# Moving small loads and rotary angles beside the feed-forward, and the key compression and key turns into the key-value stage, on one core

## The chip, the cores and the metric

One core of a Trainium2 chip. The metric is device microseconds of one execution of the whole program, lower is better.

## The reference, cut to what matters

A deep fp32 network over 512 tokens of width 1024 (P = 128 partitions, so LT = 4 token tiles). Its last layers are a forgetting attention, a feed-forward, then shared keys and values, a sparse attention that uses them, and a second feed-forward. The part that matters here is `shared_kv`, between the first feed-forward and the sparse attention:

```python
def shared_kv(h, positions, kv_norm, kv_w, kc_pe, vc_pe, kc_w1, kc_w2, vc_w1, vc_w2, kc_gain, ks_gain, kw_gain):
    hn = rms_norm_2(h, kv_norm)
    parts = (hn @ kv_w).reshape(B, T, 6, N_KV_GROUPS, HEAD_DIM)     # 512 x 1024 @ 1024 x 768
    kc_raw, vc_raw, ks, vs, kw, vw = (parts[:, :, i] for i in range(6))
    starts = arange(31) * 16; idx = starts[:, None] + arange(32)     # 31 overlapping blocks of 32 tokens
    def compress(raw, pe, w1, w2):                                   # w1: 2048 x 256, w2: 256 x 64
        blk = (raw[:, idx] + pe)...reshape(B, 31, 2, 32 * 64)
        return gelu(blk @ w1) @ w2
    kc, vc = compress(kc_raw, kc_pe, kc_w1, kc_w2), compress(vc_raw, vc_pe, vc_w1, vc_w2)
    kc = partial_rope(rms_norm_2(kc, kc_gain), positions[:, ends])
    ks = partial_rope(rms_norm_2(ks, ks_gain), positions)
    kw = partial_rope(rms_norm_2(kw, kw_gain), positions)
```

(Here cut and abridged; two groups of heads, head size 64; the rotary part covers 16 of the 64.)

## The kernel before, in words

The program is a long row of stages. Each `Stage` opens a block with one instruction stream per engine (SP issues transfers, PE multiplies, ACT, DVE and POOL do the rest); the streams meet at its end, and the next stage starts after that. Within a stream the order is the order of the code; engines wait for each other on semaphores. `Chain` lets DVE wait for its own last instruction.

After the first feed-forward (`conv_ffn`, layer 0) `sparse_attention` (L3619) runs these stages in turn:

1. `vector_steps` at L3660: a memset of the positions.
2. `load_all` (L86): SP issues seven small loads (positions twice, inverse frequencies, signs, the compression's position terms `cmp_pe`, a mask, a bias) and the first two landings of `kv_w` (an `Early` object); ACT's queue issues the compression's weights `cmp_w` (two of 2048 KB, two of 64 KB). The stage ends when the seven small loads have landed.
3. `rope_from_positions` (L3392): twelve small DVE steps make the angles, ACT looks up sine twice, one DVE step puts the signs on.
4. `normed_linear` (L625) for `kv_w`: ACT squares and takes roots of the rows of x, DVE normalizes them, PE turns them, ACT and DVE make a high and a low part (fp32r) of the turned rows and of each 256-wide piece of the weights; PE multiplies hi*hi, hi*lo, lo*hi. Pieces 0 and 1 are the token-major columns 256 to 767 (keys and values, `KS`, `VS`, `KW`, `VW`), piece 2 the feature-major raw columns 0 to 255 that the compression needs. `hi_part`, `lo_part`, `keep_unit`, `head_square`, `head_sum`, `head_scale`, `head_rope` are its steps; per-head norm and rotary of KS and KW come in the loop over pieces and after it, with POOL multiplying the gains.
5. `load_all` (call at L3684): two transfers inside SBUF swap halves of `raw`, so that both groups lie on both halves of the partitions.
6. `compress` (L3443): sixteen DVE adds (L3474) lay out the blocks; PE (L3495) multiplies with the weights `w1` as the stationary side (128 columns) and the blocks as the moving side (62 columns), into `cmp_ps`; ACT takes gelu; then two small products into `kc_ps` and `vc_ps`.
7. `head_norm` (L1039) of the compressed keys.
8. `turn_stacks` (L1195): POOL doubles each of six key stacks into `twice`, PE turns them (L1231), ACT and DVE make hi and lo.
9. `normed_linear` for `b_w_in`, the projection of the sparse attention; not touched, but for what comes below.

`conv_ffn` (L3244) has a norm stage (`norm_turn`, whose SP stream issues the `Early` loads) and a main stage of 66 chunks: 44 up (UP = 44) and 22 down. For chunk c + 2 ACT makes the high part of the weights (L3324) and DVE the low part (L3346), after PE has used chunk c - 1; PE multiplies chunk c. In the up part DVE also convolves and ACT takes silu.

In `mixture`, an earlier stage that the prediction uses for a price, L1982 multiplies fp32 with a stationary side of 64 columns, the two halves of the array's columns in turn, and a moving side of 512.

## Time and profile before

| what | value |
|---|---|
| median of 3 runs | 4573.47 us (4568.03 to 4594.96) |
| the profiled execution's own time | 4570.35 us |
| its span, first to last instruction | 4568.5 us |
| PE busy | 3857.8 us, 84% of the span |
| DVE busy | 2038.3 us, 45% |
| ACT busy | 1082.4 us, 24% |
| POOL busy | 561.4 us, 12% |
| mean granted TensorE clock | 0.898 |

Times of the trace are us from the span's start. A busy share is a mean over stages that have different limits, so the table says little of a change to one stage; the time lines of that stage do. The time of the profiled execution is 1.85 us more than its span.

### The profile page before, as it was taken

To read this page: it belongs to the slowest core of one execution; us is meant where nothing else is said; L and a number is where in the kernel's file an instruction comes from. 1 tells how busy PE (TensorE), PEld (TensorE's weight loads), DVE (VectorE), ACT (ScalarE), POOL (GpSimd) and SP (SyncE) were. 2 spreads that over 40 slices of the span, in tenths; PEclk is the share of its full clock that TensorE was granted. 3 is DMA by queue.
4 is the path that set the end of the run, shared out by engine and by line. 5 is a ranking of instruction groups with operands and counts; after the bars stand their busy time and mean duration, and the time that the engine had idled before them with its cause. 6 is when DMAs were issued, how large, how long until landed. Compare 5 with 4: busy or idle time off the path is not lost. (4 is left out here: it accounts for less than half of the span.)

```text
span 4568.5 us, 70879 instructions
## 1 busy us (share of the span) xinstructions
PE 3857.8 (84%) x29878; PEld 2815.9 (62%) x29878; DVE 2038.3 (45%) x3790; ACT 1082.4 (24%) x2119; POOL 561.4 (12%) x626
## 2 busy tenths in 40 slices
PE   6878876999978797979977877798899958798998
PEld 4645673444448674868953222396688748686877
DVE  3268953000044456756542000256477244554762
ACT  2122322000023413222111000225322122472221
POOL 0011000111102202414200000014000000250000
PEclk8987787999989997969788999999899977699999
DMA  4241017999951211000049999820122221002222
GB/s 153 85 156 30 1 61 315 383 395 389 396 168 54 88 64 39 3 1 3 2 156 399 397 401 401 327 75 20 56 96 93 79 72 39 19 2 76 95 93 79
DMA packets 194619, 657.94 MB, mean 144 GB/s; under 512 B 27544, under 2 KB 85912, under 8 KB 144620
## 3 DMA queue, kind: packets, MB, share of 16 engines
q1 hardware_dynamic: 176576, 613.95, 35.7%
q0 software_dynamic: 13056, 35.14, 2.9%
q8 instruction: 238, 3.90, 0.4%
q10 hardware_dynamic: 4672, 4.33, 0.3%
q14 instruction: 77, 0.63, 0.0%
HBM read 624.44 MB, written 28.39 MB: 143 GB/s over the span
## 5 line engine op out<-in xcount | busy, mean ns | idle before, releaser
L3346 DVE TENSOR_TENSOR w_lo<-ffn_landing,w_hi 128x1024 fp32r<-128x1024 f32 x132 | 161.4, 1225 | 293.3 <-ACT w_hi L3324 293.3
L3298 PE MATMUL ffn_ps<-ffn_inT_hi,w_hi 128*128 128x512 f32 x704 | 276.0, 392 | 9.3 <-DVE w_lo L3346 9.3
L3298 PE MATMUL ffn_ps<-ffn_inT_lo,w_hi 128*128 128x512 f32 x704 | 275.5, 391 | 0.0
L3298 PE MATMUL ffn_ps<-ffn_inT_hi,w_lo 128*128 128x512 f32 x704 | 275.3, 391 | 0.0
L1982 PE MATMUL up_ps<-w_quarter,rowsT 128*64 128x512 f32 x1024 | 237.2, 606 | 36.7 <-DMA w_quarter<-in_moe_w 36.7
L1982 PE MATMUL gate_ps<-w_quarter,rowsT 128*64 128x512 f32 x1024 | 237.0, 608 | 30.9 <-DMA w_quarter<-in_moe_w 22.2
L1982 PE MATMUL down_ps<-w_quarter,hiddenT 128*64 128x512 f32 x1024 | 235.2, 599 | 30.6 <-DMA w_quarter<-in_moe_w 28.5
L1898 POOL DMA_INDIRECT summed_dram<-gains_then_rows,part_row x48 | 74.8, 1559 | 932.3 <-DVE gains_then_rows L2112 927.4
L1982 PEld LDWEIGHTS down_ps<-w_quarter,hiddenT 128*64 128x64 f32 x1024 | 68.5, 136 | 188.4 <-issue 129.6
L2105 DVE TENSOR_TENSOR gain_then_hidden<-up_ps,gain_then_hidden 128x768 f32<-128x768 f32 (+1 forms) x32 | 26.4, 825 | 351.5 <-PE up_ps L1994 179.6
L1982 PEld LDWEIGHTS up_ps<-w_quarter,rowsT 128*64 128x64 f32 x1024 | 68.6, 138 | 182.7 <-issue 111.1
L3324 ACT ACTIVATE w_hi<-ffn_landing 128x1024 fp32r<-128x1024 f32 x132 | 138.1, 1049 | 181.5 <-PE ffn_ps L3311 163.4
L1982 PEld LDWEIGHTS gate_ps<-w_quarter,rowsT 128*64 128x64 f32 x1024 | 69.6, 139 | 178.6 <-issue 119.0
L2042 ACT ACTIVATE rowsT<-misc_ps 128x384 f32<-128x384 f32 (+1 forms) x64 | 27.8, 438 | 599.7 <-PE misc_ps L1971 598.0
L2112 DVE SCALAR_TENSOR_TENSOR gains_then_rows<-down_ps,part_gates,row_gain 128x512 f32<-128x512 f32 (+1 forms) x48 | 30.3, 659 | 308.6 <-PE down_ps L1994 170.1
L2098 DVE COPY hiddenT<-misc_ps 128x512 f32<-128x512 f32 (+1 forms) x48 | 27.4, 599 | 309.6 <-PE misc_ps L2012 309.6
L3298 PEld LDWEIGHTS ffn_ps<-ffn_inT_hi,w_hi 128*128 128x128 f32 x704 | 133.2, 189 | 37.5 <-DVE w_lo L3346 9.8
L3298 PEld LDWEIGHTS ffn_ps<-ffn_inT_hi,w_lo 128*128 128x128 f32 x704 | 133.1, 189 | 28.0
L3298 PEld LDWEIGHTS ffn_ps<-ffn_inT_lo,w_hi 128*128 128x128 f32 x704 | 133.2, 189 | 27.7
L1525 ACT ACTIVATE probT<-probT_ps 128x384 f32<-128x384 f32 (+3 forms) x256 | 112.0, 451 | 96.3 <-PE probT_ps L1483 94.7
L1656 DVE SCALAR_TENSOR_TENSOR mla_in<-mixedT,cv_w,mla_in 128x512 f32<-128x512 f32 x240 | 130.8, 612 | 0.0
L2773 PE MATMUL x_ps<-X_blocks,prod 64*64 64x64 f32 x1728 | 124.9, 229 | 5.6 <-ACT prod L2486 4.5
(693 smaller groups left out, 8831.5 us busy)
## 6 DMA issues: line engine op xcount, KB each, us to landing
w_quarter<-in_moe_w SPq DMA_DIRECT2D x384, 1024.0 KB, 17.4
ffn_landing<-in_f_w_up SPq DMA_DIRECT2D x88, 512.0 KB, 3.5
ada_ring<-in_ada_w SPq DMA_DIRECT2D x80, 512.0 KB, 5.2
ffn_landing<-in_f_w_down SPq DMA_DIRECT2D x44, 512.0 KB, 3.5
w_landing<-in_od_w_in SPq DMA_DIRECT2D x13, 1024.0 KB, 10.4
w_landing<-in_a_w_in SPq DMA_DIRECT2D x12, 1024.0 KB, 5.2
ada_landing<-in_ada_w SPq DMA_DIRECT2D x8, 1024.0 KB, 12.6
w_landing<-in_ev_w_in SPq DMA_DIRECT2D x6, 1024.0 KB, 5.2
```

Of the source, the lines that this page charges most:

```text
L1525: nc.scalar.activation(pT[:, i % ST, a:b], pt[k % 2][:, 0:b - a], ACT.Copy).then_inc(tkept, 1)
L1656: ins = nc.vector.scalar_tensor_tensor(out=to, in0=src, scalar=w[:, c, j:j + 1], in1=to, op0=ALU.mult, op1=ALU.add)
L1898: nc.gpsimd.indirect_dma_start(out=to, out_offset=bass.IndirectOffsetOnAxis(ap=pidx[:, part, e:e + 1], axis=0), in_=ys[e % 2][:, cols], in ...
L1982: mm = nc.tensor.matmul(out[n * 64:(n + 1) * 64, 0:LW], v[:, k, 0:LR], land[c][:, kk, n * LW:(n + 1) * LW], start=(k == 0), stop=(k == KD ...
L2042: nc.scalar.activation(xs[:, half * HK:(half + 1) * HK, :], misc[half][:, 0:HK * R].rearrange("p (k r) -> p k r", k=HK), ACT.Copy).then_in ...
L2098: nc.vector.tensor_copy(hT[:, :, r0:r0 + r].rearrange("p (n j) r -> p j n r", n=n), misc[part][:, 0:KD * r].rearrange("p (j n r) -> p j n ...
L2105: tt(hid[:, 0:W], p3[:, 0:W], hid[:, 0:W], ALU.mult).then_inc(hid_ready, 1)
L2112: last = nc.vector.scalar_tensor_tensor(out=ys[e % 2][:, cols], in0=py[:, cols], scalar=gall[:, part, e:e + 1], in1=g2r[:, cols], op0=ALU. ...
L2773: mm(bx[g][hb, cols], Pm[g][hb, q, :], X[g][hb, q, :], start=True, stop=True, skip_group_check=True)
L3298: mm = nc.tensor.matmul(ps[c % 4][:, :], w[:, c % NP, cols], h[:, k, :], start=(k + i == 0), stop=(k == KD - 1 and i == 2))
L3324: nc.scalar.activation(wh[:, c % NP, :], land[:, c % NL, :], ACT.Copy).then_inc(hi_ready, 1)
L3346: nc.vector.tensor_tensor(wl[:, c % NP, :], land[:, c % NL, :], wh[:, c % NP, :].bitcast(F32), ALU.subtract).then_inc(split, 1)
```

## The change

- A new class `Positions` makes the buffers and the memset before the first feed-forward. Its seven small loads are issued by SP in that feed-forward's norm stage, behind the four early weight landings (`Together`); the angle steps run on DVE behind the low part of chunk UP + 6 (loop index UP + 4), the two sine look-ups on ACT at UP + 6, the signs on DVE at UP + 10.
- `vector_steps`, `load_all` and `rope_from_positions` go from between the feed-forward and the key-value stage. `kv_w` and the compression's weights are loaded by SP inside that stage: pieces 0 and 1, the four loads of `guest.load`, then piece 2.
- The order of pieces is KS/VS, raw, KW/VW. `keep_raw` makes four copies of 64x512 per unit in place of two, straight to both halves, into the spare rows of x; the two swapping transfers go.
- A new class `Compress` is a guest of `normed_linear`: three memsets on DVE at the start (`clear`), the sixteen block adds on DVE after the keeps of piece 1 (`blocks`), doubling on POOL between the gains, and PE, ACT and DVE parts behind the stage's own. The first product has the sides swapped: blocks stationary (64 columns, the two inputs on the two halves of the array's columns), `w1` moving (256 columns), 32 products in place of 64. The hidden rows are then turned twice. The norm and rotary of the compressed keys (all on DVE but the root), and the six key turns, are inside too. `compress`, this use of `head_norm`, and `turn_stacks` for the keys go.
- `head_rope` gets one semaphore increment, in every `normed_linear` with rotary heads.

```diff
                 sp.dma_start(land[:, c % RING, :, 0:b - a], wv[:, :, job[1] + a:job[1] + b]).then_inc(landed[c % RING], 16)
+                if guest is not None and c == RING - 1:
+                    guest.load(sp)
...
+                if guest is not None:
+                    guest.double(pool, i)
...
+            if guest is not None:
+                guest.double_compressed(pool)
...
+                guest.tensor(pe)
...
+                guest.scalar(act)
...
+                    dve.sem_inc(head_roped, 1)
...
+                guest.clear(chain)
             for i in range(3):
...
+                if guest is not None and c == guest.after:
+                    guest.blocks(dve, kept, u)
                 lo_part(c + RING)
                 head_sum(c - 1)
                 head_scale(c - 2)
...
+                guest.vector(dve, chain)
...
+                  early=early if side is None else Together(early, side))
...
+                if side is not None and c == UP + 6:
+                    side.look_up(act)
...
+                if side is not None and c == UP + 4:
+                    side.angles(dve, chain)
+                if side is not None and c == UP + 10:
+                    side.signs(dve, chain)
...
+        self.pairs = [(pos[:, 0:LT], d["positions"].rearrange("(t p) -> p t", p=P)),
+                      (pos[0:NCMP, LT:n], d["positions"][31:SEQ:16].unsqueeze(1)),
+                      (self.inv[:, :], d["inv_freq"].partition_broadcast(P)),
+                      (self.sign[:, :], d["sin_sign"].partition_broadcast(P)), (self.pe_c[:, :, :], d["cmp_pe"]),
+                      (self.mask[:, :, :], d["cmp_mask"]), (self.bias[:, :], d["b_gate"].partition_broadcast(P))]
+        vector_steps(nc, lambda chain: nc.vector.memset(pos[:, :], 0))
...
+    def look_up(self, act):
+        act.wait_ge(self.ready, 1)
+        self.nc.scalar.activation(self.cos[:, :, :], self.b[:, :, :], ACT.Sin)
+        self.nc.scalar.activation(self.sin[:, :, :], self.a[:, :, :], ACT.Sin).then_inc(self.looked, 1)
...
+    def load(self, sp):
+        for dst, src in self.loads:
+            sp.dma_start(dst, src).then_inc(self.landed, 16)
+
+    def clear(self, chain):
+        chain(self.nc.vector.memset(self.blk[:, :, :, :, :], 0.0))
+        self.nc.vector.memset(self.zc, 0.0)
+        chain(self.nc.vector.memset(self.vb, 0.0))
...
+        ins.then_inc(self.ready, 1)
+
+    def double(self, pool, head):
+        if head == 0:
+            pool.wait_ge(self.ready, 1)
+        pool.wait_ge(self.roped, head + 1)
+        for i in (2 * head, 2 * head + 1):
+            src = self.stacks[i][0]
+            self.nc.gpsimd.tensor_copy(self.dup[i], src.unsqueeze(2).broadcast_to([P, LT, 2, 64])).then_inc(self.doubled, 1)
+
+    def double_compressed(self, pool):
+        pool.wait_ge(self.normed, 1)
+        for g in range(2):
+            pool.wait_ge(self.sturned, g + 1)
+            self.nc.gpsimd.tensor_copy(self.dup[g][:, 0:1], self.zc[:, 0:1, g, :].unsqueeze(2).broadcast_to([P, 1, 2, 64])) \
...
+        def stack(i):
+            n = LT if i < 4 else 1
+            pe.wait_ge(self.doubled, i + 1)
+            if i >= 2:
+                pe.wait_ge(self.skept, i - 1)
+            for t in range(n):
+                ins = turn(self.stack[i % 2][:, t * P:(t + 1) * P], self.dup[i % 4][:, t].rearrange("p y d -> p (y d)"),
+                           self.ident)
+            ins.then_inc(self.sturned, 1)
+
+        pe.wait_ge(self.landed, 16 * len(self.loads))
+        pe.wait_ge(self.ready, 1)
+        for m in range(16):
+            for s in range(2):
+                ins = mm(self.sums[64 * s:64 * s + 64, :], self.blk[:, s, m].rearrange("p g n -> p (g n)"), self.w1[:, s, m, :],
+                         start=(m == 0), stop=(m == 15), skip_group_check=True)
+        ins.then_inc(self.summed, 1)
+        stack(0)
+        pe.wait_ge(self.gelued, 1)
+        for k in range(2):
+            ins = turn(self.hidT[:, k * P:(k + 1) * P], self.gelu[:, k * P:(k + 1) * P], self.ident)
+        ins.then_inc(self.turned, 1)
+        stack(1)
...
+        pe.wait_ge(self.kept, 1)
+        for g in range(2):
             for k in range(2):
+                mm(self.out[0:32, g * 64:(g + 1) * 64], self.hid[:, k, 32 * g:32 * g + 32], self.w2[:, 0, k, :], start=(k == 0),
+                   stop=(k == 1), skip_group_check=True)
+        for g in range(2):
+            for k in range(2):
+                ins = mm(self.out[:, 128 + g * 64:192 + g * 64], self.rep[:, k, g].rearrange("p a b -> p (a b)"),
+                         self.w2[:, 1, k, :], start=(k == 0), stop=(k == 1), skip_group_check=True)
+        ins.then_inc(self.rows, 1)
+        for i in range(2, 6):
+            stack(i)
+
+    def scalar(self, act):
+        def hi(i):
+            n = (LT if i < 4 else 1) * P
+            act.wait_ge(self.sturned, i + 1)
+            to = (self.stacks + self.compressed)[i][1]
+            self.nc.scalar.activation(to, self.stack[i % 2][:, 0:n], ACT.Copy).then_inc(self.shi, 1)
+
+        act.wait_ge(self.summed, 1)
+        self.nc.scalar.activation(self.gelu[:, :], self.sums, ACT.Gelu_apprx_tanh).then_inc(self.gelued, 1)
+        hi(0)
+        hi(1)
+        act.wait_ge(self.mean, 1)
+        self.nc.scalar.activation(self.ss[:, :], self.ss[:, :], ACT.Sqrt).then_inc(self.root, 1)
+        for i in range(2, 6):
+            hi(i)
...
+        lo(0)
+        dve.wait_ge(self.turned, 1)
+        v.tensor_copy(self.hid[:, :, :].rearrange("p k n -> p (k n)"), self.hidT)
+        for k in range(2):
+            ins = v.tensor_copy(self.rep[:, k], self.hidT[:, k * P + 64:(k + 1) * P].rearrange("p (g n) -> p g n", g=2).unsqueeze(2)
+                                .broadcast_to([P, 2, 4, 32]))
+        ins.then_inc(self.kept, 1)
+        lo(1)
+        dve.wait_ge(self.rows, 1)
+        chain(v.tensor_copy(z[0:32].rearrange("p g d -> p (g d)"), self.out[0:32, 0:128]))
+        for i in range(4):
+            v.tensor_copy(self.vb[32 * i:32 * i + 32, :, 64 * i:64 * i + 64],
+                          self.out[32 * i:32 * i + 32, 128:256].rearrange("p (g d) -> p g d", g=2))
+        chain(v.tensor_tensor(self.sq[:, :, :], z, z, ALU.mult))
+        chain(v.tensor_reduce(ss, self.sq[:, :, :], AX_X, ALU.add))
+        v.tensor_scalar(ss, ss, 1.0 / 64, EPS, ALU.mult, ALU.add).then_inc(self.mean, 1)
+        dve.wait_ge(self.root, 1)
+        chain(v.reciprocal(ss, ss))
+        chain(v.tensor_tensor(z, z, ss.unsqueeze(2).broadcast_to(wide), ALU.mult))
+        chain(v.tensor_tensor(z, z, self.gain.unsqueeze(1).broadcast_to(wide), ALU.mult))
+        for y in range(2):
+            ws, other = slice(y * 8, y * 8 + 8), slice(8 - y * 8, 16 - y * 8)
+            last = v.tensor_tensor(self.rp[:, :, ws], z[:, :, other], self.sin[:, ws].unsqueeze(1).broadcast_to([P, 2, 8]), ALU.mult)
+        chain(last)
+        chain(v.tensor_tensor(z[:, :, 0:16], z[:, :, 0:16], self.cos.unsqueeze(1).broadcast_to([P, 2, 16]), ALU.mult))
+        v.tensor_tensor(z[:, :, 0:16], z[:, :, 0:16], self.rp[:, :, :], ALU.add).then_inc(self.normed, 1)
+        for i in range(2, 6):
+            lo(i)
...
-                nc.vector.tensor_copy(raw[0:64, 0, f, :], ps[0:64, :])
-                return nc.vector.tensor_copy(raw[64:P, 1, f, :], ps[64:P, :])
-
-            def keep_two(ps, chain, t, a, b):
-                for i, buf in enumerate(((KS, VS), (KW, VW))[a // 256]):
-                    ins = nc.vector.tensor_copy(buf[:, t, :], ps[:, i * P:(i + 1) * P])
+                for g in range(2):
+                    for y in range(2):
+                        ins = nc.vector.tensor_copy(raw[64 * y:64 * y + 64, g, f, :], ps[64 * g:64 * g + 64, :])
                 return ins
+
+            def keep_two(*bufs):
+                def keep(ps, chain, t, a, b):
+                    for i, buf in enumerate(bufs):
+                        ins = nc.vector.tensor_copy(buf[:, t, :], ps[:, i * P:(i + 1) * P])
+                    return ins
+                return keep
...
             normed_linear(nc, x, [(0, LT, cst["kv_norm_2"], None)], (hT, hTl), d["kv_w"],
-                          [("tok", 256, 512, tiles, keep_two), ("feat", 0, 256, [(0, SEQ)], keep_raw)], ident, heads, RING=2, early=early)
-
-            load_all(nc, [(raw[64:P, 0], raw[0:64, 0]), (raw[0:64, 1], raw[64:P, 1])])
-            compress(nc, w1, w2, cmp_landed, raw, pe_c, zc[:, :, :, :], vb[:, :, :])
-            head_norm(nc, zc[:, :, :, :], [0], 2, 64, cst["kc_gain"], rope=([0], 0, 1, 8, C[:, LT:], Sn[:, LT:]))
-            turn_stacks(nc, [(z[:, :, g * 64:(g + 1) * 64], kh[:, g, :], kl[:, g, :])
-                             for z, kh, kl in ((KS, ksh, ksl), (KW, kwh, kwl)) for g in range(2)] +
-                        [(zc[:, :, g, :], kch[:, g, :], kcl[:, g, :]) for g in range(2)], ident)
+                          [("tok", 256, 256, tiles, keep_two(KS, VS)), ("feat", 0, 256, [(0, SEQ)], keep_raw),
+                           ("tok", 512, 256, tiles, keep_two(KW, VW))], ident, heads, RING=2, guest=guest)
```

## Rows read from the trace of the kernel before

**Rows 1.** Windows view: busy us (x instructions) by engine, granted clock, DMA share, GB/s.
```profile
3672.10:3692.00 19.90, 0.00 (x0) 0.00 (x0) 2.90 (x14) 0.43 (x2) 0.00 (x0) 0.50 0.90 284
3692.00:3740.50 48.50, 42.02 (x272) 38.92 (x272) 24.72 (x65) 21.88 (x51) 0.00 (x0) 0.87 0.14 41
...
3745.00:3747.00 2.00, 0.00 (x0) 0.00 (x0) 1.97 (x4) 0.00 (x0) 1.31 (x1) 0.68 0.00 0
...
3762.70:3790.50 27.80, 27.54 (x128) 27.38 (x128) 0.00 (x0) 0.15 (x1) 0.00 (x0) 0.50 0.00 1
...
3800.10:3806.95 6.85, 4.10 (x18) 3.70 (x18) 3.16 (x6) 2.73 (x6) 2.81 (x6) 0.50 0.00 0
```

**Rows 2.** Timeline, feed-forward's end to key-value stage: start, us, operation, [idle before <-releaser].
```profile
3667.20 4.87 DVE L3386 TENSOR_TENSOR x<-x,ffn_ps 128x512 f32<-128x512 f32 x8 [13.94 <-PE ffn_ps L3311]
3672.48 0.06 DVE L3660 MEMSET positions<- 128x5 int32 x1 [0.41 <-PEq L69]
...
3687.92 0.17 DVE L3417 CAST pos_float<-positions 128x5 f32<-128x5 int32 x1 [15.38 <-PEq L69]
...
3692.03 0.06 DVE L915 MEMSET eps<- 128x1 f32 x1 [0.40 <-PEq L69]
...
3694.91 0.16 DVE L827 RECIPROCAL inverse_root<-inverse_root 128x1 f32<-128x1 f32 x1 [2.82 <-ACT inverse_root L758]
```

**Rows 3.** Timeline, projection of keys and values.
```profile
3717.82 1.12 PE L742 MATMUL lin_ps<-w_hi,hbT_hi 128*128 128x256 f32 x8
...
3729.34 2.00 PE L742 MATMUL lin_ps<-hbT_hi,w_hi 128*128 128x512 f32 x8
...
3740.45 0.68 DVE L3670 COPY cmp_raw<-lin_ps 64x512 f32<-64x512 f32 x1 [4.05 <-PE lin_ps L742]
```

**Rows 4.** Timeline, norm and rotary of the two key heads.
```profile
3742.90 0.69 DVE L899 TENSOR_TENSOR k_sel<-k_sel,head_roots 128x512 f32<-128x512 f32 x1
...
3743.68 1.26 POOL L695 TENSOR_TENSOR k_sel<-k_sel,ks_gain 128x512 f32<-128x512 f32 x1 [523.43 <-DVE k_sel L899]
3743.74 1.75 DVE L899 TENSOR_TENSOR k_win<-k_win,head_roots 128x512 f32<-128x512 f32 x1
...
3747.38 0.36 DVE L908 TENSOR_TENSOR rope_part<-k_win,pos_sin 128x64 f32<-128x64 f32 x2
...
3748.10 0.29 DVE L913 TENSOR_TENSOR k_win<-k_win,rope_part 128x128 f32<-128x128 f32 x1
```

**Rows 5.** Timeline, compression and the compressed keys' norm and rotary.
```profile
3754.30 0.48 DVE L3466 MEMSET v_cmp<- 128x512 f32 x1
3754.82 7.81 DVE L3474 TENSOR_TENSOR blocks<-cmp_raw,cmp_pe 64x248 f32<-64x248 f32 x16
...
3762.78 27.54 PE L3495 MATMUL cmp_ps<-blocks,cmp_w 128*128 128x62 f32 x128 [22.36 <-DVE blocks L3474]
...
3792.44 1.97 PE L3506 MATMUL vc_ps<-cmp_w,cmp_hidden 128*128 128x64 f32 x8
3794.45 0.28 DVE L3484 COPY k_cmp<-kc_ps 32x128 f32<-32x128 f32 x1 [3.05 <-PE vc_ps L3506]
...
3799.90 0.19 DVE L1132 TENSOR_TENSOR k_cmp<-k_cmp,squares 128x32 f32<-128x32 f32 x1
```

**Rows 6.** Timeline, end of the key turns and start of the next projection.
```profile
3806.46 0.48 DVE L1250 TENSOR_TENSOR k_cmp_lo<-stack_ps,k_cmp_hi 128x128 fp32r<-128x128 f32 x2
...
3807.37 0.06 DVE L915 MEMSET eps<- 128x1 f32 x1 [0.43 <-PEq L69]
```

**Rows 7.** Timeline, PE in the mixture: 64-column stationary sides on alternating halves.
```profile
770.85 4.51 PE L1982 MATMUL up_ps<-w_quarter,rowsT 128*64 128x512 f32 x20
```

**Rows 8.** Timeline, DVE in the feed-forward's down part; such a row every 5.44 us.
```profile
3564.99 1.23 DVE L3346 TENSOR_TENSOR w_lo<-ffn_landing,w_hi 128x1024 fp32r<-128x1024 f32 x1 [4.21 <-ACT w_hi L3324]
```

**Rows 9.** DMA view: issues after the feed-forward; last number is median us to landing.
```profile
kv_w_landing<-in_kv_w SPq DMA_DIRECT2D x3, 1024.0 KB, 12.2
...
cmp_w<-in_vc_w ACTq DMA_DIRECT2D x1, 2048.0 KB, 21.6
```

More of the change, by code:

```diff
@@ L238, in load_first, with __init__ @@
             eng.dma_start(self.land[:, i], src).then_inc(self.landed[i], 16)
+class Together:
+    def __init__(self, *parts):
+        self.parts = parts
+    def load_first(self, eng):
+        for part in self.parts:
+            part.load_first(eng)
 class Ahead:
@@ L622, in _, with normed_linear @@
                     then()
-def normed_linear(nc, x, segments, h, w, jobs, ident, heads=(), RING=3, beside=(), early=None, arrived=None):
+def normed_linear(nc, x, segments, h, w, jobs, ident, heads=(), RING=3, beside=(), early=None, arrived=None, guest=None):
     hh, hl = h
@@ L746, in _ @@
                     u += 1
+            if guest is not None:
+                guest.tensor(pe)
         @block.scalar
@@ L818, in _ @@
                 head_roots(c - RING - 1)
+            if guest is not None:
+                guest.scalar(act)
         @block.vector
@@ L949, in _ @@
             head_rope(n - 1)
+            if guest is not None:
+                guest.vector(dve, chain)
             if order:
@@ L3616, in _, with sparse_attention @@
                 nc.vector.tensor_copy(dst, src)
-def sparse_attention(nc, d, x, cst):
+def sparse_attention(nc, d, x, cst, side):
     ident = cst["ident"]
@@ new lines, in sparse_attention @@
+            stacks = [(z[:, :, g * 64:(g + 1) * 64], kh[:, g, :], kl[:, g, :])
+                      for z, kh, kl in ((KS, ksh, ksl), (KW, kwh, kwl)) for g in range(2)]
+            compressed = [(zc[:, :, g, :], kch[:, g, :], kcl[:, g, :]) for g in range(2)]
+            guest = Compress(nc, ident, w1, w2, loads, raw, side.pe_c, zc[:, :, :, :], vb[:, :, :], cst["kc_gain"], C[:, LT], Sn[:, LT],
+                             stacks, compressed)
+            normed_linear(nc, x, [(0, LT, cst["kv_norm_2"], None)], (hT, hTl), d["kv_w"],
+                          [("tok", 256, 256, tiles, keep_two(KS, VS)), ("feat", 0, 256, [(0, SEQ)], keep_raw),
+                           ("tok", 512, 256, tiles, keep_two(KW, VW))], ident, heads, RING=2, guest=guest)
@@ L3765, in build @@
         forgetting(nc, d, x, cst, arrived[1])
-        conv_ffn(nc, d, 0, x, cst)
-        sparse_attention(nc, d, x, cst)
+        with ExitStack() as c1:
+            side = Positions(nc, c1, d)
+            conv_ffn(nc, d, 0, x, cst, side)
+            sparse_attention(nc, d, x, cst, side)
         conv_ffn(nc, d, 1, x, cst)
```

237 lines of the change are left out of this document (104 added, 133 removed).

## The prediction
> **What bounds the kernel now.** I read the page's totals first: PE is busy 84% of 4568.5 us. That says nothing of the place of the change, so next come the windows and the timeline between the feed-forward's last add and the next projection. The reader is to see that PE, the busiest engine overall, does nothing for most of that stretch. The last add ends at 3672.07 (3667.20 + 4.87), the first instruction of the next `normed_linear` starts at 3807.37 [rows 2, 6]: 135.3 us. It divides so:
> - 3672.07 to 3692.03, 20.0 us: PE has no instruction. DVE waits 15.38 us for the stage of the small loads to end, while DMA runs at 284 GB/s [rows 1, 2]. What is moving is mostly `kv_w` and `cmp_w`; seven tiny loads share the transfer engines with 4 MB and hold up everyone.
> - 3692.03 to 3740.4, 48.4 us: the projection, PE busy 42.02 us [rows 1, 3]. This is real work.
> - 3740.4 to 3807.37, 67.0 us: a serial tail, of which 27.5 us is the first compression product, at granted clock 0.50, i.e. 1.2 GHz [rows 1, 5].
> So the stretch is bounded by latency and order, by no engine's rate.
>
> **The change, part by part.** Times below count from the eps memset that opens the key-value stage (0 = 3692.03 before, 3672.5 after).
>
> *Front.* The small loads, angles and signs go; the projection starts one stage change after the last add. A stage change is the 0.41 us of the positions' memset [rows 2]. Gain 3692.03 - 3672.48 = 19.55 us. The memset's own stage only moves ahead of the first feed-forward: minus 0.45 (0.41 + 0.06). Net 19.1.
>
> *What the feed-forward takes on.* Angles, look-ups, signs and the stage change after them took 4.1 us in all (3687.92 to 3692.03 [rows 2]), the DVE steps up to the look-ups about 3 of it; these come behind the low part of a down chunk, where DVE sits idle 4.21 us of every 5.44 [rows 8]. The low parts run two chunks ahead of PE, so even an overrun of one chunk is covered. ACT's look-ups and DVE's sign step are shorter. The small loads are issued behind four early landings, more than 40 chunks before they are used. Cost 0; without cover it would be 3 to 5 us once.
>
> *Loads in the stage.* `kv_w` now starts with the stage. Median landing of its MB was 12.2 us beside `cmp_w` and the last 2 MB of `cmp_w` took 21.6 us [rows 9], at 284 GB/s [rows 1]. Alone at that rate 1 MB takes 3.7 us; piece 0 lands near 5, piece 1 near 9, the 4.2 MB of the guest near 24, piece 2 near 28. Piece 0 is wanted only when the first rows are normed (from 2.9 on: 3694.91 [rows 2]), turned and split, about 7.5; the guest's at 48. Piece 2 is queued behind the guest's loads on SP: ACT could start on it at 25.8 (when piece 0's products end, 3717.82 [rows 3]), and with 2 + 2.3 us of splitting PE needs it started by 32.5, since piece 1 lasts to 36.8. I take 0; bounds 0 and +10, if it lands at 38.
> The clearing memsets are 128x2048 and 128x512: 0.48 us per 512 columns [rows 5] makes 2.4 us, inside the 2.82 us that DVE waits for ACT's first root [rows 2]. Cost 0.
>
> *Projection.* Same products: piece 0 ends at 25.8; raw takes 11.0 (3729.34 to 3740.4); the other tokens piece 11.5 (3717.82 to 3729.34) [rows 3]. PE ends at 48.3 as before. Raw now needs four copies of 0.69 per unit, 2.8 us, less than the unit's 5.5: kept at 39.8. The sixteen adds, 7.8 us [rows 5], end at 47.6, before PE is done. So copies, swapping transfers, their stage and the adds leave the path.
>
> *First product.* Before: 128 instructions in 27.54, 215 ns each [rows 5]. After: 64 instructions with a 64-column stationary side on alternating halves and 256 moving columns. The same form with 512 columns ran at 4.51 / 20 = 0.2255 us each [rows 7]; half is 0.113, times 64 = 7.2 us at 2.4 GHz. At 1.2 GHz 14.4; if the halves did not overlap either, 28.9, which is the upper bound (nothing gained). I take 7.2, as PE comes straight from dense work: after PE's last product the clock was still above its low level in 3745 to 3747 (0.68) [rows 1], five us later. PE then ends at 55.5.
> The Trainium skill (TensorE: Matmul & The Clock Gate, "The mechanism") says a weight load overlaps running products only when its row group differs; all 64 loads here use all rows, and by its LDWEIGHTS formula 64 columns cost 53 ns, so by that rule 3.4 us come on top. The row speaks against: 0.2255 exceeds 512/2.4 GHz = 0.213 by 12 ns only.
>
> *Heads on DVE, which sets the end.* One pass over 128x512 is 0.69 [rows 4], by which I size the others. After the adds (47.6): sum of the first head 0.9; last four keeps, eight copies of 128x128, 1.7, to 50.2; scale 0.9, to 51.1; second sum 0.9, to 52.0; POOL's gain 1.26 runs to 52.4; first rotary 1.0 (3747.38 to 3748.39), to 53.4; second scale 0.2 + up to 1.75, as it falls beside POOL [rows 4], to 55.3; gain 1.3, to 56.6; second rotary to 57.7. PE's product has long ended, its gelu and two turns too (56.7).
>
> *Rest, on a DVE-PE-DVE chain.* First low part 0.7 and three copies of 0.4: 59.6. Sixteen small products: about 3.0 us at 1.2 GHz (1.97 for the last eight [rows 5], about 1 for the eight with a quarter of the weights), half at 2.4; 1.7 taken: 61.3. Then copies, norm and rotary: before from 3794.45 to 3800.09, 5.6 us with two stage changes and a POOL step [rows 5]; without them about 4.1: 65.4. Doubling, low parts of the last stacks, one turn each for the compressed keys, which alternate on two banks: 2.5. End 67.9, next eps memset 0.43 later [rows 6]: 68.3. Before it was 3807.37 - 3692.03 = 115.3. The tail gains 47.0.
> The key turns of the heads (before a stage of 6.85 us [rows 1]) fit beside this chain.
>
> *Added wait.* POOL's doublings stand between the gains, so the second gain waits for them; 1.2 us, in the chain above. The extra increment in `head_rope` is below 0.1 us.
>
> *Sum.* 19.1 + 47.0 = 66.1 us off. I take 2 off for some twenty semaphore hops at 0.1: 64. Against the profiled execution, 4570.35 - 64 = 4506. That execution lies 3 us under the median of the runs; from the median, 4573.47 - 64 = 4509.5. I say 4509.
>
> **Rivals.**
> 1. *The product runs at 1.2 GHz* or without overlap. For: it was at 0.50 for 27.5 us although PE was busy throughout [rows 1]; and the adds might end after the projection. Against: the moving side is now 256 columns. Costs 7.2, and DVE's later start on the hidden rows absorbs 1 to 2, the small products give 1.5: about 7 worse, 4516. With no overlap too, 21 worse: 4530.
> 2. *DVE is late or piece 2 is.* The adds sit ahead of the keeps and head sums on DVE. If copies into the other half of the partitions or work beside POOL take double (1.75 against 0.69 [rows 4]), the chain grows by 8 to 12; a late piece 2 adds up to 10. 4517 to 4530. For: the 1.75 row. Against: only few steps meet POOL.
> 3. *Slower: the feed-forward loses its clock.* If the angle steps or look-ups starve PE at chunk UP + 4 long enough for the clock to fall, and it stays at 0.50 as in the compression, each of the 18 remaining down chunks takes 10.9 in place of 5.44 us: +98, minus 64, 4607. It decides from 12 such chunks on (64 / 5.44). For: a busy PE stayed at the low clock for 27 us [rows 1]. Against: DVE's idle 4.21 us holds the 3 us of steps, and two chunks are ready ahead [rows 8].
> 4. *It doesn't do what it says:* the stage's loads delay piece 0 and the wait only moves: 19 minus 12 left of the front, both rivals above beside it, so 4535 to 4550.
>
> **How the numbers follow.** Forecast 0.65; rival 1 0.13; rival 2 0.13; rival 4 0.06; rival 3 0.03. No measurement of this kernel tells less than about 1% (46 us) from no change. The likeliest case's saving is over it, and so are rivals 1 and 2 but for their last part (2 in 26 of them within); rival 4 is within. Faster 0.88, within 1% 0.09, slower 0.03. Range: 4496 (every step without hops, the front whole, 10 us of noise in the run) to 4528, which takes in most of rivals 1 and 2.
>
> **What the profile will show.** Right: no gap between the last add and the eps memset beyond 0.5 us; a first product of 64 instructions in about 7 us at clock 1.00, starting within 1 us of the projection's end; 68 us from eps to eps; the feed-forward's DVE low parts still every 5.44 us. Wrong: PE waits for a landing or for `blocks`; the product at 0.50; a second POOL gain that ends after 58; an ACT or DVE step in the feed-forward that PE waits for.

## The result, and the profile after

The changed kernel took 4529.74 us (median of four executions, 4508.55 to 4536.52) beside 4579.94 for the kernel before in the same session: ratio 0.9897, 95% interval 0.9861 to 0.9934. The forecast was 4509, with a range of 4496 to 4528; the measured median lies 1.7 us above it. With the unchanged copies that ran later there are twelve executions of the changed kernel (4493.71 to 4536.52, median 4511.5, mean 4513.7) and fifty-three of the kernel before (4552.46 to 4596.20, median 4568.0, mean 4573.4). The difference of the means is 59.7 us; the mean of twelve is itself uncertain by 4.5 (its standard error). In the first session the kernel before had its median 6.5 us above the 4573.47 from which the forecast counted, and the saving was 50.2 us for the 64 forecast.

The totals of the profiled execution (4525.77 us):

```profile
span 4523.9 us, 70660 instructions
PE 3847.8 (85%) x29816; PEld 2812.7 (62%) x29816; DVE 2041.8 (45%) x3795; ACT 1082.0 (24%) x2118; POOL 560.5 (12%) x625
```

They say nothing of the change, as before. The windows of the place itself do (columns: window, PE, PEld, DVE, ACT, POOL busy, granted clock, DMA share, GB/s); they answer to [rows 1]:

```profile
3693.60:3694.10 0.50, 0.00 (x0) 0.00 (x0) 0.10 (x2) 0.00 (x0) 0.00 (x0) 0.50 0.00 0
3694.10:3742.20 48.10, 41.29 (x272) 38.17 (x272) 36.84 (x80) 21.11 (x49) 0.00 (x0) 0.88 0.50 156
3742.20:3749.40 7.20, 7.20 (x67) 4.59 (x66) 6.56 (x20) 2.33 (x4) 2.68 (x3) 1.00 0.01 2
3749.40:3763.90 14.50, 6.91 (x36) 5.43 (x36) 8.67 (x28) 4.59 (x9) 3.14 (x6) 0.64 0.00 1
```

The 20 us without a PE instruction are 0.4, the projection is the same 48, the product is 7.2 us at full clock where it was 27.8 at half, and 14.5 us of chain follow. The transfers, 0.90 of the engines for 20 us before, are now 0.50 beside the projection. The last add ends at 3688.78 + 4.87 = 3693.65, and the next projection opens at 3763.91:

```profile
3688.78 4.87 DVE L3424 TENSOR_TENSOR x<-x,ffn_ps 128x512 f32<-128x512 f32 x8 [13.94 <-PE ffn_ps L3343]
3694.06 0.06 DVE L940 MEMSET eps<- 128x1 f32 x1 [0.40 <-PEq L69]
...
3697.11 0.16 DVE L851 RECIPROCAL inverse_root<-inverse_root 128x1 f32<-128x1 f32 x1
...
3763.91 0.06 DVE L940 MEMSET eps<- 128x1 f32 x1 [0.42 <-PEq L69]
```

So the stretch from the last add to the next projection is 70.3 us against 135.3 [rows 2, 6]: 65.0 off, and 69.85 from eps to eps where 68.3 were forecast. But the two spans differ by only 4568.5 - 4523.9 = 44.6. The missing 20.4 lie elsewhere, 17.2 of them in one stage that the change does not touch: the first direction of the recurrent layer, which ends some 1660 us earlier. Windows from state memset to state memset, then to the second direction's end; first the kernel before:

```profile
1747.20:2011.40 264.20, 231.61 (x4384) 209.87 (x4384) 160.29 (x309) 70.61 (x164) 88.84 (x90) 0.85 0.01 2
2011.40:2290.80 279.40, 248.00 (x4384) 226.34 (x4384) 167.70 (x321) 69.92 (x165) 89.05 (x90) 0.79 0.01 2
```

and the changed kernel:

```profile
1747.90:2029.30 281.40, 249.08 (x4384) 227.43 (x4384) 159.55 (x310) 70.55 (x164) 88.67 (x90) 0.79 0.01 2
2029.30:2308.70 279.40, 248.02 (x4384) 226.40 (x4384) 167.67 (x321) 69.88 (x165) 89.04 (x90) 0.79 0.01 2
```

In the first direction the same 4384 PE instructions ran one time at a mean granted clock of 0.85 and one time at 0.79.

### The profile page after: what moved, and what is told of

Read it like the earlier page. It is cut to its first block and busy times, and to the rows that moved or that the text cites. A ratio compares the mean times of both kernels' runs of the same rounds, so it can differ in the third digit from the quotient of the medians.

```text
span 4523.9 us, 70660 instructions
## 1 busy us (share of the span) xinstructions
PE 3847.8 (85%) x29816; PEld 2812.7 (62%) x29816; DVE 2041.8 (45%) x3795; ACT 1082.0 (24%) x2118; POOL 560.5 (12%) x625
## 5 line engine op out<-in xcount | busy, mean ns | idle before, releaser
L2013 PEld LDWEIGHTS up_ps<-w_quarter,rowsT 128*64 128x64 f32 x1024 | 68.3, 138 | 181.7 <-issue 110.0
L2073 ACT ACTIVATE rowsT<-misc_ps 128x384 f32<-128x384 f32 (+1 forms) x64 | 27.8, 437 | 599.3 <-PE misc_ps L2002 597.6
L3330 PEld LDWEIGHTS ffn_ps<-ffn_inT_lo,w_hi 128*128 128x128 f32 x704 | 133.3, 189 | 27.8
L3330 PEld LDWEIGHTS ffn_ps<-ffn_inT_hi,w_lo 128*128 128x128 f32 x704 | 133.3, 189 | 27.5
## 6 DMA issues: line engine op xcount, KB each, us to landing
ada_landing<-in_ada_w SPq DMA_DIRECT2D x8, 1024.0 KB, 12.4
```

The costliest lines, as they stand in the source:

```text
L2013: mm = nc.tensor.matmul(out[n * 64:(n + 1) * 64, 0:LW], v[:, k, 0:LR], land[c][:, kk, n * LW:(n + 1) * LW], start=(k == 0), stop=(k == KD ...
L3330: mm = nc.tensor.matmul(ps[c % 4][:, :], w[:, c % NP, cols], h[:, k, :], start=(k + i == 0), stop=(k == KD - 1 and i == 2))
```

## The experiments

Two questions were open. Is the gain made of the parts that the prediction named? And is the missing part a consequence of the change or a scatter of that other stage? For the second, three numbers of each profile are set side by side: the two directions of the recurrent layer, the stretch behind the feed-forward, and the rest of the span.

**The changed kernel once more** (no edit).

> The changed kernel, unaltered. In its first profile the key-value stretch (last add of the feed-forward to the next eps memset) took 70.3 us, 65.0 less than before, yet the span fell by 44.6 only, because direction 0 of the recurrent stage, whose code did not change, took 281.4 us in place of 264.2. Theory A (that stage's clock falls as chance has it, the same in both kernels): over several runs the saving comes to 60 to 66 us, and a profile again shows 70 us in the stretch. Theory B (the change makes the earlier stages some 18 us slower each time): the saving stays at 45 to 50 us and direction 0 takes 281 us again.

Measured: 4509.36 us median of six, ratio 0.9876 (0.9848 to 0.9903); profile span 4502.4, directions 266.5 and 266.8, stretch 70.4. The stretch is the same within 0.2, the first direction 15 us shorter, and the median lies 60.4 us under the kernel before in the same session, inside Theory A's 60 to 66. So the 17 us of the first profile are no fixed price of the change, as Theory B had it.

**Small loads and angles back in stages of their own**, between the feed-forward and the key-value stage, everything else as changed:

```diff
-            conv_ffn(nc, d, 0, x, cst, side)
+            conv_ffn(nc, d, 0, x, cst)
+            side.alone()     # stage 1: load_first and its wait; stage 2: angles, look_up, signs
```

> The changed kernel, but small loads, angles, look-ups and signs in two stages of their own between the feed-forward and the key-value stage; the big loads stay where the change put them. Theory A (the small loads were held up by the 4 MB that moved beside them): the stretch grows by 11 to 14 us against the changed kernel's 70.3. Theory B (the small loads are slow by themselves, for their many tiny packets): it grows by the 19.5 us that the front had before.

Measured: 4514.7 us, ratio 0.9883 (0.9854 to 0.9912), stretch 80.5, 10.2 longer than with them beside the feed-forward. That is a little less than Theory A's 11 to 14 and far from Theory B's 19.5. The front by itself, between the last add's end at 3665.78 and the eps memset, first SP's queue:

```profile
3666.11 0.79 SPq L3459 DMA_DIRECT2D positions<-in_positions  x2
...
3668.75 0.43 SPq L3459 DMA_DIRECT2D branch_bias<-in_b_gate  x1
```

and DVE, from the start of the angles:

```profile
3672.15 0.17 DVE L3494 CAST pos_float<-positions 128x5 f32<-128x5 int32 x1 [6.37 <-PEq L69]
...
3676.46 0.06 DVE L940 MEMSET eps<- 128x1 f32 x1 [0.61 <-DVE pos_sin L3515]
```

The loads by themselves hold everybody for 6.37 us where they took 15.38 with the large weights beside them [rows 2]: two landings of `kv_w` and all of `cmp_w`, some 6 MB in all, of which the prediction and this expectation count 4. So of the 19.6 us that the front lost, about 9 were the company of the large weights, 6 the small loads' own latency and some 4 the angle steps.

**The first product with its old sides** (weights stationary, 128 instructions, hence no turns of the hidden rows) at its new place:

```diff
-        for m in range(16):
-            for s in range(2):
-                ins = mm(self.sums[64 * s:64 * s + 64, :], self.blk[:, s, m]..., self.w1[:, s, m, :], ...)
+        for s in range(2):
+            for ht in range(2):
+                for m in range(16):
+                    ins = mm(self.sums[:, (2 * ht + s) * 64:(2 * ht + s + 1) * 64],
+                             self.w1[:, s, m, ht * P:(ht + 1) * P], self.blk[:, s, m]..., ...)
```

> The changed kernel, but the first compression product with w1 stationary again (128 instructions with 64 moving columns; no turns of the hidden rows). It follows the dense projection, at the high clock. Theory A (the instruction form sets the granted clock, so it falls a few us in): the product takes 20 to 27 us, the stretch grows by 12 to 19. Theory B (coming warm is enough, 215 ns per instruction halve): 13.7 us, the stretch grows by 4 to 6.

Measured: 4511.71 us, ratio 0.9887 (0.9854 to 0.992), stretch 74.5, 4.2 longer. PE's timeline, from the projection's last products:

```profile
3718.14 1.11 PE L762 MATMUL lin_ps<-w_hi,hbT_lo 128*128 128x256 f32 x8
3719.09 14.40 PE L3584 MATMUL turn_ps<-blocks,cmp_w 128*128 128x64 f32 x128
...
3735.95 0.63 PE L3594 MATMUL turn_ps<-cmp_w,cmp_hidden 128*32 128x64 f32 x8 [1.33 <-DVE cmp_hidden L3634]
3736.51 1.44 PE L3598 MATMUL turn_ps<-cmp_w,cmp_hidden 128*128 128x64 f32 x8
```

and its window:

```profile
3719.00:3733.30 14.30, 14.30 (x131) 14.30 (x130) 7.61 (x24) 2.33 (x4) 5.28 (x6) 1.00 0.01 2
```

The very form that ran at 0.50 for 27.5 us [rows 5] stays at 1.00 when PE comes to it straight from the projection: Theory B. Half of the old price was the clock that PE had at its start and kept. The form takes 7.2 us more than the new one at the same clock, and the path sees 4.2 of them. In this window the weight loads (PEld) are busy for all of the 14.30 us, in the changed kernel's for 4.59 of 7.20; so the old form, with a load of 128 columns for every 64 moving ones, is most likely paced by its loads.

**The other way about: only the sides swapped**, in the kernel before, in the compression's own stage, reached after PE had been idle for 24 us:

> The kernel before, with only the sides of the first compression product swapped, in its own stage, after 22 us of an idle TensorE. Theory A (this form brings the clock up as in the mixture, where it rose 4 to 5 us after the start): 64 instructions in about 10 us. Theory B (it stays at the low clock as the old form did): 14.4 us. In both the stretch falls by the difference to 27.5, less about 1 us for the two turns: 12 to 17 us of the 135.3.

Measured: 4549.32 us, ratio 0.9955 (0.9934 to 0.9976), stretch 119.9, 15.4 shorter than before. PE's timeline:

```profile
3754.08 9.85 PE L3493 MATMUL cmp_ps<-cmp_w,blocks 128*64 128x256 f32 x64 [24.24 <-DVE blocks L3472]
3764.41 0.44 PE L3498 MATMUL cmp_turn_ps<-ident,cmp_gelu 128*128 128x128 f32 x2 [0.47 <-ACT cmp_gelu L3514]
3766.02 0.63 PE L3503 MATMUL kc_ps<-cmp_w,cmp_hidden 128*32 128x64 f32 x8 [1.18 <-DVE cmp_hidden L3479]
3766.59 1.10 PE L3507 MATMUL vc_ps<-cmp_w,cmp_hidden 128*128 128x64 f32 x8
```

It starts cold (mean clock 0.72) and still needs 9.85 instead of 27.54, as Theory A forecast: with 256 moving columns the clock came up during the product. Position and form thus remedy in large part the same loss; together they give 20.4 us of PE time, and neither is worth its lone price once the other is there (17.7 for the form alone, 13.1 for the position alone).

**A shorter chain at the end**: the compressed keys' small products write to a part of PSUM of their own and release DVE before those of the values run; the hidden copies go ahead of the first two low parts, the value copies behind the fourth. (Only the first of these edits is shown.)

```diff
+        self.kout = banks[1][:, 256:384]
...
-                mm(self.out[0:32, g * 64:(g + 1) * 64], self.hid[:, k, 32 * g:32 * g + 32], ...)
+                ins = mm(self.kout[0:32, g * 64:(g + 1) * 64], self.hid[:, k, 32 * g:32 * g + 32], ...)
+        ins.then_inc(self.rows, 1)
```

> The changed kernel with its last chain re-ordered: the eight small products of the compressed keys write to a part of PSUM of their own and release DVE at their end, so that the norm of the compressed keys no longer waits for the eight products of the compressed values; the copies of the hidden rows stand ahead of the first two doublings' low parts, and the copies of the values behind all of them. In the changed kernel's profile these eight products took 1.97 us at granted clock 0.50 and the copies and low parts that move out of the way about 1.5 us. Theory A (the end of the stretch is set by the chain hidden rows, small products, norm): eps to eps falls from 69.85 to 66 to 67 us and the time by 3 to 4 us under the changed kernel. Theory B (the stretch ends with PE's or POOL's own queue): eps to eps stays within 0.7 of 69.85.

Measured: 67.04 us from eps to eps, 2.8 less, at the edge of the 66 to 67 of Theory A. PE's timeline:

```profile
3746.65 0.95 PE L3596 MATMUL turn_ps<-cmp_w,cmp_hidden 128*32 128x64 f32 x8 [2.44 <-DVE cmp_hidden L3636]
3747.54 1.97 PE L3601 MATMUL turn_ps<-cmp_w,cmp_hidden 128*128 128x64 f32 x8
```

and DVE's:

```profile
3747.71 0.27 DVE L3642 COPY k_cmp<-turn_ps 32x128 f32<-32x128 f32 x1
...
3750.47 0.19 DVE L3655 TENSOR_TENSOR k_cmp<-k_cmp,cmp_rope 128x32 f32<-128x32 f32 x1
```

The norm now runs beside the values' products. The chain hidden rows, small products, norm does set the end. Yet the whole kernel gave 4518.7 us (4493.55 to 4532.85, six executions), ratio 0.9876 (0.9834 to 0.9917). The 3 to 4 us under the changed kernel that Theory A also forecast do not show; 3 us cannot be told from nothing here, so it is the better version by its trace alone.

**Both kernels again, for the scatter.**

> The kernel before, unchanged, for another profile of it. Theory A (the first direction of the recurrent stage scatters by itself in both kernels): it takes anything from 264 to 282 us here too, and the span less the two directions and less the stretch behind the feed-forward stays at 3890 us within 3. Theory B (the change lengthened that stage): 264 to 265 us again, while unchanged copies of the changed kernel lie higher.

> The changed kernel, unchanged, for a third profile. Theory A (the recurrent stage scatters by itself): directions between 264 and 282 us; span less both directions and less the stretch 3890 within 3, the stretch 70.3 within 0.3. Theory B (the change lengthened the stage): the first direction near 281 us.

Measured: the kernel before 4564.18 us (median of eight), ratio to its other executions 1.0003 (0.997 to 1.0035), directions 266.5 and 279.4, stretch 135.0. The changed kernel 4496.24 (two executions), ratio 0.9836 (0.9779 to 0.9893), directions 264.3 and 262.5, stretch 70.2. All profiles with an unchanged recurrent layer:

```
kernel           span    direction 1, 2   stretch  rest of the span
before           4568.5  264.2  279.4     135.3    3889.6
before again     4573.2  266.5  279.4     135.0    3892.2
sides alone      4542.3  265.9  266.9     119.9    3889.6
changed          4523.9  281.4  279.4      70.3    3892.8
changed again    4502.4  266.5  266.8      70.4    3898.7
changed third    4491.9  264.3  262.5      70.2    3894.9
late positions   4510.1  272.4  266.8      80.5    3890.4
old sides        4510.9  266.5  279.4      74.5    3890.5
rows first       4520.6  281.6  279.6      67.4    3892.0
```

The rest is constant within 9 us; the two directions together range over 526.8 to 561.2. Theory A of both expectations holds but for two figures: the third profile's second direction, 262.5, lies 1.5 us under its range, and its rest, 3894.9, 2 us over. Theory B wanted a first direction near 281 us in the changed kernel each time, and it took 266.5 and 264.3. One thing stays open: in none of the three profiles with the old key-value stage was the first direction long, and in three of the six with the new one it was (272.4, 281.4, 281.6), which is too few to tell the two apart. Nineteen of the fifty-three executions of the kernel before took 4582 to 4596 us, the others 4552 to 4575; none of the nineteen was profiled, so whether their first direction was long is not known.

The lengths come in three groups, and the record of the granted clock says why. In all of these profiles the clock is at 0.50 for most of a direction's first 45 us and its last 20. Besides that and some short falls, a direction has one, two or three stretches of 14 to 17 us at 0.50 inside its chunks: one in the ten directions of 262.5 to 266.9, two in the one of 272.4, three in the seven of 279.4 to 281.6. When the first of them comes early (130 to 132 us after the start), two more follow, each some 44 us later at the same place of the next chunk. Two more stretches of 17.1 us at half the clock lose 17.1 us, which is the difference of 17.2 between the first two profiles.

What does PE do before such a fall? At the end of a chunk it waits twice, once before the solve (L2695) and once before the update of the state (L2704). The first profile of the changed kernel, where the clock falls at 1879.5, between the start of the one and of the other, then a window from there to the end of the chunk's output products:

```profile
1877.28 1.97 PE L2695 MATMUL side_ps<-rhs,XT 128*128 128x64 f32 x16 [0.99 <-issue]
1879.93 0.49 PE L2704 MATMUL side_ps<-sa,B_rows 128*64 128x64 f32 x4 [0.69 <-ACT sa L2510]
1879.50:1892.30 12.80, 12.37 (x80) 12.16 (x80) 3.49 (x10) 0.38 (x1) 0.00 (x0) 0.50 0.01 1
```

and the same 80 instructions in its third profile:

```profile
1878.24 1.97 PE L2695 MATMUL side_ps<-rhs,XT 128*128 128x64 f32 x16 [0.99 <-issue]
1880.89 0.34 PE L2704 MATMUL side_ps<-sa,B_rows 128*64 128x64 f32 x4 [0.69 <-ACT sa L2510]
1880.90:1887.50 6.60, 6.60 (x80) 6.49 (x80) 3.10 (x9) 0.00 (x0) 0.00 (x0) 1.00 0.01 2
```

The instructions and the two waits are the same; one time the clock falls and the 80 instructions take 12.4 us, the other time it stays and they take 6.6. All thirty-three long stretches of the eighteen directions begin at this place, thirty of them ahead of the first output product and three with it, after PE has been idle for 0.8 to 1.75 of the last 5 us. So the waits go before every fall, but they do not bring one each time.

**Does the start of a direction decide?** Six dense products ahead of each, in PE's idle time:

```diff
+            for i in range(6):
+                mm(bx[i % 2][:, :], ident, V[:, 0, :], start=True, stop=True, skip_group_check=True)
             for s in range(NCHUNK):
```

> The changed kernel with six extra products of 128x128 by 128x512 (fp32, result thrown away) at the start of each of the two directions of the recurrent stage, where PE idles 11.88 us before its first product; nothing else differs, and no result changes. In the profiles so far the first direction took 264.2 to 281.4 us and the second 266.8 or 279.4, with the same instructions. Theory A (the two directions' scatter comes from the state of the clock at their start): both directions become alike, near 262 us or below in every execution, and the first products (42 in 1.66 us at clock 0.50) take about half. Theory B (the falls in the middle come by themselves, wherever a chunk's end meets them): the first products take half, 1 to 5 us are gained at the start of each direction, and the falls to 0.50 within the chunks appear as before, so the directions still scatter by 13 to 17 us.

Measured: 4512.29 us, ratio 0.9865 (0.9818 to 0.9911). The windows of the two directions:

```profile
1749.80:2020.20 270.40, 244.97 (x4396) 218.89 (x4396) 160.25 (x310) 70.57 (x164) 88.78 (x90) 0.84 0.01 2
2020.20:2286.10 265.90, 241.54 (x4396) 215.72 (x4397) 166.91 (x321) 69.91 (x165) 88.88 (x90) 0.85 0.01 2
```

and PE's timeline at the first one's start:

```profile
1773.75 7.46 PE L2769 MATMUL x_ps<-v_rows,ident 128*128 128x512 f32 x12 [2.51 <-PEq L69]
1783.13 0.99 PE L2683 MATMUL x_ps<-mixedT 64*64 64x64 f32 x42 [1.91 <-POOL K L2467]
```

The first products take 0.99 us instead of 1.66, but two stretches of 17 us appear in the first direction and one in the second. That is Theory B: a warm start does not keep the falls away. (The rest of the span was 3904.4 here, above every profile of the table; the cause of that is open.)

**Are thin products behind it?** The expectation takes the falls to begin among the output products of a chunk (128 weight columns for 64 moving ones); by the record of the clock thirty of the thirty-three begin just ahead of them. One dense product behind each of their four groups therefore stands inside the stretch at 0.50, and ahead of the next chunk's waits:

```diff
                             ins = mm(hv(m[1], h), QB[h % 2][:, j, :], hv(sa, h), start=False, stop=True, ...)
+                        mm(bp[j % 2][:, 0:512], ident, V[:, c, 0:512], start=True, stop=True, skip_group_check=True)
```

> The changed kernel with one extra product of 128x128 by 128x512 (fp32, result thrown away) behind each of the four groups of output products of a chunk in the recurrent stage; the falls of the granted clock to 0.50 begin in those groups, whose products have 128-column weights and only 64 moving columns. No result changes. At full clock one extra product takes 4 x 512 / 2.4 GHz = 0.85 us, so the four chunks with outputs of each direction pay 3.4 us each, 27 us for both. Theory A (the falls come from those thin products): the clock stays at 1.00 through the chunks in every execution, the falls' cost of 9 to 26 us per direction goes, and the two directions take about the same in the profile as in the best execution seen (264.3 and 262.5) plus 14 each less the falls that even that one had, 265 to 275 each, alike. Theory B (the falls come by something else): they appear as before, and both directions grow by about 14 us over a range of 262 to 281.

Measured: 4514.76 us (4504.94 to 4525.24), ratio 0.9859 (0.9806 to 0.9912). The windows of the two directions:

```profile
1742.30:2013.00 270.70, 239.06 (x4416) 207.96 (x4416) 159.48 (x309) 70.62 (x164) 88.68 (x90) 0.89 0.01 2
2013.00:2285.60 272.60, 241.79 (x4417) 211.81 (x4417) 166.65 (x322) 69.90 (x165) 88.95 (x90) 0.87 0.01 2
```

Both directions are alike and in the forecast 265 to 275; the mean clock is the highest of all profiles, and no stretch at 0.50 inside the chunks is longer than 10.2 us, where each of the eighteen unchanged directions had one of 14 to 17. The clock did not stay at 1.00 as Theory A wanted: in the second direction it fell for 10.2 us at 211 us from the start, behind the same two waits, and came back sooner. A part of the higher mean comes from the ends of the directions, where it also came back after 10.2 us. What this saves the dense products spend: the median stays where it was.

> As the kernel with a dense product of 512 columns behind each group of output products, but with 256 columns: the price at full clock is 14 us for both directions. Theory A (the falls come from thin products): fewer falls than in the unchanged directions, which took 262 to 282 us in ten profiles; both directions at or below 265. Theory B: falls as before, directions 269 to 288.

With 256 columns: 4517.03 us (4507.63 to 4532.04), ratio 0.9849 (0.9797 to 0.9902), directions 273.6 and 278.4, rest of the span 3907.8, the highest of all. Inside its chunks the first direction has two stretches at 0.50, of 10.2 us each, and the second two, of 17.1 and 20.5. By its numbers this is Theory B's range, by the first direction's short stretches it is not.

The two kernels together speak for this: dense work behind the waits makes a fall shorter, and thin work lets it last. That is supported, not settled, with one profile of each. What starts a fall they do not show. In both kernels every fall of 10 us or more inside the chunks still begins behind the two waits, no run takes the waits away, and so the waits stand untested as the cause, as does whatever makes an execution meet an early stretch.

## Why the prediction was right or wrong

*The front.* Right: 0.40 us between the last add and the eps memset, 19.6 gained.

*The feed-forward.* Right: it takes 395.8 us against 395.9, and its low parts still come every 5.44, the angles sitting between them on DVE:

```profile
3592.02 1.23 DVE L3380 TENSOR_TENSOR w_lo<-ffn_landing,w_hi 128x1024 fp32r<-128x1024 f32 x1 [4.21 <-ACT w_hi L3356]
3593.16 0.17 DVE L3471 CAST pos_float<-positions 128x5 f32<-128x5 int32 x1
...
3595.93 0.20 DVE L3483 TENSOR_SCALAR angle<-angle 128x80 f32<-128x80 f32 x1
3597.46 1.23 DVE L3380 TENSOR_TENSOR w_lo<-ffn_landing,w_hi 128x1024 fp32r<-128x1024 f32 x1 [1.32 <-ACT w_hi L3356]
```

DVE's idle time before the next low part falls from 4.21 to 1.32 [rows 8]. Rival 3 did not happen.

*Loads.* Right at 0. Piece 2's high part waited last for PE and not for its landing, and starts 25.8 us after eps, as forecast. The clearing memsets cost 0.2: the first reciprocal is at 3.05 after eps against 2.88 before [rows 2]. ACT's row for piece 2:

```profile
3719.88 1.92 ACT L789 ACTIVATE w_hi<-w_landing 128x2048 fp32r<-128x2048 f32 x1 [5.04 <-PE lin_ps L762]
```

*First product.* Right: 7.13 us at 1.00 behind the projection, forecast 7.2. Loads of the stationary side cost next to nothing: the moving columns alone take 6.83, an estimate from 64 x 256 / 2.4 GHz. By the Trainium skill's rule on row groups (TensorE: Matmul & The Clock Gate, "The mechanism") an estimated 3.4 us would have come on top; the trace does not agree with it for this form. (The same section also lets a load into the background weight buffer go ahead, which no run here can tell.) Rival 1 did not happen, and the run with the old sides kept the clock at 1.00 even without the swap. PE's timeline, with the small products that come next:

```profile
3742.26 7.13 PE L3583 MATMUL turn_ps<-cmp_w,blocks 128*64 128x256 f32 x64
...
3753.78 1.06 PE L3595 MATMUL turn_ps<-cmp_w,cmp_hidden 128*32 128x64 f32 x8 [3.03 <-DVE cmp_hidden L3635]
3754.77 1.97 PE L3599 MATMUL turn_ps<-cmp_w,cmp_hidden 128*128 128x64 f32 x8
```

*Heads on DVE.* Right in the sum: the second rotary ends at 57.8 after eps (forecast 57.7), the copies of the hidden rows at 59.7 (59.6). Inside, the second scale took 0.97 and not up to 1.75, and POOL's doublings 1.63 and not 1.2, so DVE stood 1.74 waiting for the second gain, as the part on the added wait had it. DVE's timeline:

```profile
3748.18 0.97 DVE L923 TENSOR_TENSOR k_win<-k_win,head_roots 128x512 f32<-128x512 f32 x1
3750.88 0.36 DVE L932 TENSOR_TENSOR rope_part<-k_win,pos_sin 128x64 f32<-128x64 f32 x2 [1.74 <-POOL k_win L711]
...
3752.98 0.75 DVE L3635 COPY cmp_hidden<-turn_ps 128x256 f32<-128x256 f32 x2
```

POOL's:

```profile
3747.99 1.63 POOL L3557 COPY x<-k_sel 128x512 f32<-128x512 f32 x2 [1.24 <-DVEq L938]
3749.58 1.27 POOL L711 TENSOR_TENSOR k_win<-k_win,kw_gain 128x512 f32<-128x512 f32 x1
```

Rival 2 did not happen.

*The rest of the chain.* One term mis-sized: the sixteen small products took 3.0 us, as at 1.2 GHz, for the 1.7 allowed. PE had idled 3.03 us before them and stood at 0.50; with the old sides it idled 1.33 and they took 0.63 + 1.44. With this 1.3 the measured 69.85 from eps to eps is explained to 0.3; so the 2 us set aside for semaphore hops are not seen beside it.

*The sum.* 66.1 less 2 for hops made 64; the stretch lost 65.0. The mechanism of the stretch came out in every part. That the number is so near is in part luck: the tail gained 45.5 for the 47.0 forecast, and the 2 us for hops, which did not come, stood in for the small products, which did. (In the chances, the stated split gives faster 0.89 and within 1% 0.08, not 0.88 and 0.09.)

*The step that failed* stands in the range. Its lower end has "10 us of noise in the run", its upper end, 4528, has no term for noise at all: it goes by rivals 1 and 2, neither of which happened, and still the median of four came out at 4529.74. The prediction took the rest of the program, 4435 of the 4570 us, as fixed. It is not: the recurrent layer alone varies by 34 us from profile to profile (526.8 to 561.2) with the same instructions, single executions of either kernel span 43 us, and with the twelve's standard deviation of 15.5 the mean of four is uncertain by 8. The four first ones lay high (the one profiled had three long stretches at 0.50 in both directions); all twelve have their median 2.5 us from the forecast. The three times of before, 27 us apart at an unchanged program, had shown the size, and the two directions of before, 264.2 and 279.4 us for the same 4384 products, had shown the place; the prediction never compared them. A range for four executions should have had some 15 us (twice those 8) for the scatter on either side.

## What to carry to other kernels

Set the stretch that is changed and the rest of the span side by side for both profiles before believing a total: here 65 us were gained and 17 of them hidden by a stage that ends 1660 us earlier. A small load or a small product costs what stands beside or before it: seven tiny loads waited 15 us in company and 6 alone, and a product of 128 thin instructions took 27.5 us behind an idle PE and 14.3 behind a busy one. So try such work against dense work, and in a wider shape; here either alone took most of the 20.4 us that both gave (13.1 and 17.7). And compare repeated stages of one program with each other; their spread in a single profile is the least noise that a forecast must allow. To find why a stage scatters, look at what the engine did before the clock fell, and lay the same instructions of two profiles side by side, not the same times.

## What the runs showed of the hardware

- A low clock can outlast its beginning while PE is busy: after a fall, 80 instructions with PE busy 12.37 of 12.80 us ran at 0.50; in another execution they took 6.60 us at 1.00. Before each of the thirty-three long falls inside the chunks PE had waited, 0.8 to 1.75 us out of 5. The Trainium skill (TensorE: Matmul & The Clock Gate, "HAM oscillation — how this bites in real kernels") ties such falls to waits of PE for transfers. The traces agree in that a wait goes before every long fall; here the second of the two (0.69 us) is for ACT and no transfer, and the same waits (0.99 and 0.69 us) also pass without a fall.
- One thin product kept whatever clock it met: 27.5 us at 0.50 from a cold start, 14.3 us at 1.00 from a warm one. The wide form (64 weight columns, 256 moving) came up from cold within its 9.85 us.
- The long falls repeat at the same place of successive chunks, 44 us apart, so that a direction takes one of three lengths (262 to 267, 272, 279 to 282 us) and nothing between in eighteen directions.
- 64 weight loads on alternating column halves cost 0.3 us in all over the moving columns' own time (7.13 us against an estimate of 6.83).
